# Compressing the cached pages of two sequences at a time, with the products spread over five steps

## The reference

```python
def compress(x, pe, w1, w2):              # CMP_LEN 32, CMP_STRIDE 16, hidden 128
    ch = x[:, :nch * CMP_STRIDE].reshape(N, nch, CMP_STRIDE, G, hd)
    hsum = 0
    for r in range(2):
        proj = jnp.einsum('ncsgd,sdh->ncgh', ch + pe[r][:, None, :], w1[r])
        hsum = hsum + proj[:, r:r + n_cmp]
    return jnp.einsum('ncgh,hd->ncgd', jax.nn.gelu(hsum), w2)
```

## Time and profile before

| | us |
|---|---|
| three timed runs | 1248.45, 1250.84, 1255.35 |
| their median | 1250.84 |
| the profiled execution, its own time | 1257.54 |
| its span, first to last instruction | 1255.7 |
| PE busy in the span | 1222.4 |

### The profile page before, as it was taken

How to read it: one execution, slowest core, us unless ns; L and a number is a source line. 1 busy time by engine, 2 the same in 40 slices (tenths; PEclk the granted TensorE clock), 3 DMA queues, 4 the chain that set the end, 5 groups by cost and what they waited for, 6 DMA issues and landing times.

```text
span 1255.7 us, 19647 instructions
## 1 busy us (share of the span) xinstructions
PE 1222.4 (97%) x6846; PEld 957.1 (76%) x6846; DVE 692.4 (55%) x1524; ACT 325.0 (26%) x736; POOL 281.0 (22%) x444
## 2 busy tenths in 40 slices
PE   6999999999999899999999999999999999999999
PEld 5787656878788666666787887688888888888887
DVE  6766363665655433132377724349777888873331
ACT  3422522444544422112131115221212112110000
POOL 4632002334333514214260210130101010000000
PEclk9999999999999899999999999999999999999999
DMA  6342475232333689998421731022222222302240
GB/s 228 147 175 68 138 262 184 84 103 68 89 110 128 208 300 356 305 313 306 169 102 40 296 135 34 34 68 83 85 84 84 85 69 87 143 30 93 92 159 18
DMA packets 83636, 174.59 MB, mean 139 GB/s; under 512 B 11377, under 2 KB 49074, under 8 KB 82642
## 3 DMA queue, kind: packets, MB, share of 16 engines
q1 hardware_dynamic: 67810, 123.79, 29.2%
q10 hardware_dynamic: 11568, 39.06, 8.4%
q0 software_dynamic: 4160, 10.49, 2.5%
HBM read 163.21 MB, written 10.09 MB: 138 GB/s over the span
## 4 chain that ended last, share of the span: by engine, by line
PE 89%; DVE 5%; issue 2%; ACT 2%; DMA 1%; POOL 1%; SPq 0%; ACTq 0%; DVEq 0%; POOLq 0%
PE ps L2963 20%; PE ps L3000 11%; PE ps L1865 10%; PE ps L661 7%; PE ps L1333 6%; PE ps L2674 6%; PE ps L2775 4%; PE ps L754 3%; PE ps L2687 3%; PE ps L1266 2%; PE ps L1238 2%; PE ps L1252 2%; PE ps L2823 1%; PE ps L653 1%; PE ps L1965 1%
## 5 line engine op out<-in xcount | busy, mean ns | idle before, releaser
L2963 PE MATMUL ps<-arena 128*128 128x272 f32 x1120 | 257.1, 392 | 0.7 <-DVE arena L3332 0.7
L2963 PEld LDWEIGHTS ps<-arena 128*128 128x128 f32 x1120 | 212.7, 190 | 44.9 <-DVE arena L3332 1.1
L1865 PE MATMUL ps<-arena 128*128 128x272 f32 x512 | 123.7, 399 | 0.5 <-PE ps L1965 0.5
L3000 PE MATMUL ps<-arena 128*128 128x272 f32 x528 | 121.8, 392 | 0.0
L1865 PEld LDWEIGHTS ps<-arena 128*128 128x128 f32 x512 | 97.0, 193 | 27.5 <-issue 8.3
L3000 PEld LDWEIGHTS ps<-arena 128*128 128x128 f32 x528 | 100.3, 190 | 20.7
L1333 PEld LDWEIGHTS ps<-arena 128*128 128x128 f32 x768 | 89.8, 195 | 11.9 <-issue 11.4
L1333 PE MATMUL ps<-arena 128*128 128x128 f32 (+1 forms) x768 | 95.6, 282 | 1.8 <-DVE arena L1460 1.8
L661 PE MATMUL ps<-arena 128*128 128x272 f32 x392 | 93.1, 399 | 3.4 <-POOL arena L462 3.4
L661 PEld LDWEIGHTS ps<-arena 128*128 128x128 f32 x392 | 75.2, 193 | 20.6 <-POOL arena L462 3.8
L2622 ACT ACTIVATE arena<-arena 128x560 f32<-128x560 f32 x44 | 35.3, 848 | 159.7 <-DVE arena L3347 152.9
(11 more groups left out here) (396 smaller groups left out, 1843.4 us busy)
## 6 DMA issues: line engine op xcount, KB each, us to landing
arena<-in_w_close SPq DMA_DIRECT2D x68, 512.0 KB, 3.4
arena<-in_pages_cmp SPq DMA_DIRECT2D x128, 128.0 KB, 2.1
arena<-in_past_va ACTq DMA_DIRECT2D x6, 2048.0 KB, 12.3
arena<-in_w_down SPq DMA_DIRECT2D x16, 704.0 KB, 6.0
arena<-in_past_ka ACTq DMA_DIRECT2D x6, 1792.0 KB, 10.7
arena<-in_w_close ACTq DMA_DIRECT2D x16, 512.0 KB, 6.7
arena<-in_w_proj SPq DMA_DIRECT2D x15, 512.0 KB, 3.8
arena<-in_pages_ks SPq DMA_DIRECT2D x96, 64.0 KB, 4.0
```

Of the source, the lines that this page charges most:

```text
L1865: last_one = pe.matmul(ps[:, gate_bank(q), 0:HALF], ring[:, n % CLOSE_RING, k * P:(k + 1) * P], m.h[:, k, half * HALF:(half + 1) * HALF], ...
L2963: last = pe.matmul(ps[:, bank(f, i), 0:HALF], w[:, k * P:(k + 1) * P], halved[:, rhs, k, :], start=(k == 0), stop=(k == 3))
L3000: last = pe.matmul(ps[:, down_bank(i, j), 0:HALF], w[:, k * P:(k + 1) * P], rhs[:, k, :], start=(k == 0), stop=(k == KH - 1))
```

## The change

One unit of compression is now two sequences with one `kv`: eight units for sixteen halves. A page transfer brings 64 KB (the 128 columns of one `kv`) and a unit takes 32 of them. Matmuls of EVEN and ODD have 256 columns, those of BOTH 252. ODD is accumulated on EVEN in the same half of bank 7. In between, ACT copies EVEN's result out (`take_even`) and POOL takes differences of its neighbours (`slopes`, new). `first` comes out of EVEN plus ODD by one ACT instruction (`take_first`), and `between` by two DVE instructions (`add`). The 24 matmuls of a unit are given to five steps, as 5, 3, 5, 5 and 8. Unit `n` begins in step 4 + 5n, the last ends in step 43. `bend` and `hidden` work on four rows at once. POOL's sums come in six instructions for a unit (four of 384 elements, two of 240), and stand behind the `bend` of the unit before; `next_sum` lies elsewhere. `w1` is loaded ahead of the first pages, after a wait for the prompt's last tile. The 32 page numbers of a pair of sequences are read into registers at once, ahead of the loads of its two units. Two constants of the samples' attention are loaded behind the compression, no longer ahead of the third sequence's pages.

```diff
-    chunked, next_sum = at(37944, 2, 8, 66), at(37944, 16, 64)
+    chunked, next_sum = at(37944, 2, 8, 66), at(45820, 16, 2, 64)
     w_both = at(43772, 2, 8, P)
     c_prob_t, c_score = at(39000, 2, T), at(40024, QT, 8, 32)
-    second, inner, bent = at(41048, 2, 2, P), at(41560, 2, 2, P), at(42072, 2, 2, P)
-    hid = at(42584, 2, 2, 2, P)
+    even, slope = at(41048, 4, 64), at(41304, 4, 64)
+    inner, bent = at(41560, 4, P), at(42072, 4, P)
...
-    copied = sem("sample_copied")
+    copied, slope_ready = sem("sample_copied"), m.x_root_ready
...
+
+    UNIT_STEPS = 5
+    PIECES = [[(EVEN, 0, 5)], [(EVEN, 5, 8)], [(ODD, 0, 5)], [(ODD, 5, 8), (BOTH, 0, 2)], [(BOTH, 2, 8)]]
+
+    def begin(n):
+        return 4 + UNIT_STEPS * n
+
+    def even_step(n):
+        return begin(n) + 1
+
+    def last_step(n):
+        return begin(n) + UNIT_STEPS - 1
+
+    def small_step(s):
+        return last_step(2 * (s // 2) + 1) + 3 + s % 2
+
+    def product_done(n, product):
+        return 1 + 3 * n + product + 1
...
+        return product_done(2 * (s // 2) + kv, BOTH)
...
-    def part(product):
-        return ps[:, PROJ, P * product:P * product + P].rearrange("p (g i) -> p g i", g=2)
-
-    def page_view(s, kv):
-        return pages[:, s % 2].rearrange("p n (v a w i) -> p v w a n i", v=2, a=16, w=2)[:, kv]
+    def slot(product):
+        at_ = 256 * (product == BOTH)
+        return ps[:, PROJ, at_:at_ + 256].rearrange("p (x i) -> p x i", x=4)
+
+    def page_view(n):
+        return pages[:, n % 2].rearrange("p n (a w i) -> p w a n i", a=16, w=2)
+
+    def windows(kv):
+        return hid[:, kv].rearrange("p x (i w) -> p w x i", w=2)
...
+        def pages_of(q):
+            found = []
+            for p4 in range(2 * NPAGE // 4):
+                at = 2 * q * NPAGE + 4 * p4
+                _, four = nc.values_load_multi_w_load_instructions(
                     table[0:1, at:at + 4], engines=(mybir.EngineType.SP,), min_val=0,
                     max_val=d["pages_cmp"].shape[0] - 1)
-                for c, page in enumerate(found):
-                    sp.dma_start(pages[:, s % 2, 4 * p4 + c, :],
-                                 d["pages_cmp"][ds(page, 1)].rearrange("a p n -> p (a n)"))\
-                        .then_inc(page_in[s % 2], 16)
+                found += four
+            return found
+
+        def load_pages(n, found):
+            _, kv = PAIRS[n]
+            for c, page in enumerate(found):
+                sp.dma_start(pages[:, n % 2, c, :],
+                             d["pages_cmp"][ds(page, 1), :, P * kv:P * kv + P].rearrange("a p n -> p (a n)"))\
+                    .then_inc(page_in[n % 2], 16)
...
         sp.wait_ge(m.z_full, m.products_done)
-        load_pages(0)
+        found = pages_of(0)
+        sp.wait_ge(m.tile_done, m.NJOB)
+        sp.dma_start(w1, d["w_cmp1"]).then_inc(w_in, 16)
+        load_pages(0, found)
         m.store_tiles(sp)
-        sp.dma_start(w1, d["w_cmp1"]).then_inc(w_in, 16)
         m.store_values(sp)
-        load_pages(1)
+        load_pages(1, found)
         sp.wait_ge(m.stored, 16 * 7)
         sp.wait_ge(m.h_scaled, QT + 1)
-        m.load_constants(sp)
-        for s in range(2, NSEQ):
-            sp.wait_ge(proj_full, products(s - 2, 1))
-            load_pages(s)
+        for n in range(2, len(PAIRS)):
+            if n % 2 == 0:
+                found = pages_of(n // 2)
+            sp.wait_ge(proj_full, product_done(n - 2, BOTH))
+            load_pages(n, found)
...
-        sums(*HALVES[0])
+        def sums(n):
+            pool.wait_ge(page_in[n % 2], 16 * 2 * NPAGE * (n // 2 + 1))
+            if n == 0:
+                pool.wait_ge(m.h_scaled, QT + 1)
+            else:
+                pool.wait_ge(proj_full, product_done(n - 1, BOTH))
+            x = page_view(n)
+            to = next_sum.rearrange("p a s (n i) -> p a (s n) i", i=4)
+            for a in range(0, 16, 4):
+                rows = slice(a, a + 4)
+                pool.tensor_tensor(to[:, rows, :, 0:3], x[:, 0, rows, :, 1:4], x[:, 1, rows, :, 0:3], ALU.add)
+            by_seq = x.rearrange("p w a (s n) i -> p w a s n i", s=2)
+            to = next_sum.rearrange("p a s (n i) -> p a s n i", i=4)
+            for a in range(0, 16, 8):
+                rows = slice(a, a + 8)
+                last = pool.tensor_tensor(to[:, rows, :, 0:NPAGE - 1, 3], by_seq[:, 0, rows, :, 1:NPAGE, 0],
+                                          by_seq[:, 1, rows, :, 0:NPAGE - 1, 3], ALU.add)
+            last.then_inc(chunked_ready, 1)
+
+        def slopes(n):
+            pool.wait_ge(second_ready, 2 + 2 * n + 1)
+            if n >= 1:
+                pool.wait_ge(proj_free, 2 + n)
+            pool.tensor_tensor(slope[:, :, 0:63], even[:, :, 0:63], even[:, :, 1:64], ALU.subtract)\
+                .then_inc(slope_ready, 1)
+
         for kv in range(2):
             bend(p_hid[:, kv, :, 0:C], p_inner[:, kv, :, 0:C], kv + 1)
-        for n, (s, kv) in enumerate(HALVES):
-            if n + 1 < len(HALVES):
-                sums(*HALVES[n + 1])
-            bend(hid[:, s % 2, kv, :, 0:NCMP_S], inner[:, kv, :, 0:NCMP_S], 2 + n + 1)
+        sums(0)
+        for n, (q, kv) in enumerate(PAIRS):
+            slopes(n)
+            if n >= 1:
+                pool.wait_ge(hid_ready, 2 + n)
+            bend(hid[:, kv, :, 0:NCMP_S], inner[:, :, 0:NCMP_S], 2 + n + 1)
+            if n + 1 < len(PAIRS):
+                sums(n + 1)
+        pool.wait_ge(proj_full, product_done(len(PAIRS) - 1, BOTH))
...
-            act.activation(bent[:, kv, :, 0:NCMP_S], inner[:, kv, :, 0:NCMP_S], ACT.Tanh, scale=GELU_IN)\
+        def take_even(n):
+            act.wait_ge(proj_full, product_done(n, EVEN))
+            if n >= 1:
+                act.wait_ge(slope_ready, SLOPE0 + n)
+            act.copy(even[:, :, :], slot(EVEN)).then_inc(second_ready, 1)
+
+        def take_first(n):
+            q, kv = PAIRS[n]
+            act.wait_ge(proj_full, product_done(n, BOTH))
+            if q >= 1:
+                act.wait_ge(s_full, s_index["small", 2 * q - 1] + 1)
+            act.activation(windows(kv)[:, 0], slot(ODD), ACT.Identity, bias=m.cmp_bias[:, kv:kv + 1])\
+                .then_inc(second_ready, 1)
+
+        def bend(n):
+            act.wait_ge(inner_ready, 2 + n + 1)
+            if n >= 1:
+                act.wait_ge(hid_ready, 2 + n)
+            act.activation(bent[:, :, 0:NCMP_S], inner[:, :, 0:NCMP_S], ACT.Tanh, scale=GELU_IN)\
                 .then_inc(bent_ready, 1)
 
...
+                    if small_step(s) == t:
                         small(s)
-                    for kv in range(2):
-                        if last_step(s, kv) + 1 == t:
-                            bend(s, kv)
-                for s in range(NSEQ):
-                    for kv in range(2):
-                        if last_step(s, kv) == t:
-                            second_half(s, kv)
+                for n in range(len(PAIRS)):
+                    if even_step(n) == t:
+                        take_even(n)
+                    if last_step(n) == t:
+                        take_first(n)
                 if 0 <= t - 2 < U:
                     take_turned(t - 2)
+                for n in range(len(PAIRS)):
+                    if last_step(n) + 1 == t:
+                        bend(n)
...
+        def piece(n, product, from_, to):
+            q, kv = PAIRS[n]
+            x = page_view(n).rearrange("p w (e s) n i -> p w s e n i", e=2)
+            follows = next_sum.rearrange("p (e s) q i -> p s e q i", e=2)
+            if from_ > 0:
+                pass
+            elif product == EVEN:
+                pe.wait_ge(proj_free, 2 + n)
+                if n >= 1:
+                    pe.wait_ge(second_ready, 2 + 2 * n)
+                pe.wait_ge(page_in[n % 2], 16 * 2 * NPAGE * (n // 2 + 1))
+            elif product == ODD:
+                pe.wait_ge(second_ready, 2 + 2 * n + 1)
+            else:
+                pe.wait_ge(chunked_ready, 10 + n + 1)
+            for s1 in range(from_, to):
+                if product == BOTH:
+                    out = slot(BOTH).rearrange("p (e q) i -> p e q i", e=2)[:, :, :, 0:63]
+                    last = pe.matmul(out, w_both[:, kv, s1, :], follows[:, s1, :, :, 0:63], start=(s1 == 0), stop=(s1 == 7))
+                else:
+                    last = pe.matmul(slot(product), w1[:, kv, product, s1, :], x[:, product, s1],
+                                     start=(product == EVEN and s1 == 0), stop=(s1 == 7),
+                                     skip_group_check=(product == ODD))
+            if to == 8:
                 last.then_inc(proj_full, 1)
...
-            pe.wait_ge(hid_ready, 2 + 2 * s + 2)
+            pe.wait_ge(hid_ready, 2 + 2 * (s // 2) + 2)
...
+                n, place = divmod(t - begin(0), UNIT_STEPS)
+                if 0 <= n < len(PAIRS):
+                    for product, s0, s1 in PIECES[place]:
+                        piece(n, product, s0, s1)
...
```

(50 more changed lines are left out.)

81 lines of the change are left out of this document (20 added, 61 removed).

## The result

The changed kernel takes 1268.62 us (median of 5 runs, 1256.08 to 1270.68) against 1253.23 for the kernel before (5 runs, 1248.45 to 1255.35). The ratio is 1.0111, with a 95% interval from 1.0087 to 1.0136: 1.1% slower, where the forecast was 1240, or 0.9% faster.

A forecast was written before the change was run, and what follows sets the result against it. PE's own work was taken to bound the kernel (busy 1222 of 1256 us). Products -7.0, loop waits 0, pages +0.5, loop end -7.2, late keys +2.7 gave -11.0: 1250.8 to 1239.8, forecast 1240; own range 1234 to 1244, all cases 1232 to 1251.

The forecast's parts named there:

- What is late next: Samples' attention behind the loop: PE 13.7 us earlier, SP's chain 2.7 earlier, 8.3 to spare; PE waits 2.7 for second keys.
- The third rival: SP's queue becomes the bound through slower page transfers, 17 us more, 1257; chance 0.08.
- The products: Compression matmuls on PE: 384 records at 0.216 us, 82.8 instead of 89.8, saving 7.0 us.
- The second rival: Wide operand or new waits eat the products' gain and the loop's end stays as it is: 1250; chance 0.22.
- Waits inside the loop: PE's gaps in the steady loop stay as before: 0 in the sum, between 3 us lost and 4.4 won.
- ODD's wait for `take_even`: In a unit's third step, where the second is 512 wide (steps 15 and 35): some 1.1 us, twice.
- the wait for `add`: PE's wait in the loop, 1.8 us in all, gets cheaper with 12 records ahead of it instead of 16 short ones.
- On DVE and ACT: Both engines in the loop: fewer instructions per unit than two halves had, busy about half the time, priced at nothing.
- The end of the loop: Around steps 43 and 44: PE's 2.6 us gap and the low clock's 4.6 us both go, saving 7.2 us.
- The pages, the stores, `w1`: Page waits at units 4 and 6 cost 0.5 us; moved stores and earlier `w1` ahead of the loop cost nothing.
- SP's pace in the loop: SP's issues and number reads for a pair of sequences take 43 us, against 45.4 for two units.

The follow-up runs named there:

- the long execution: Trace of the changed kernel rerun with nothing edited, the shortest execution of that rerun; span 1261.4 us.
- 8: Changed kernel with 32 page numbers of the samples' attention read into SP's registers ahead of the wait for unit 6; 1253.38 us, ratio 1.0009.
- 11: Changed kernel without POOL's four large sums in units 1 to 7 (output not the reference's); 1257.53 us, ratio 1.0046.
- 7: Kernel before, with SP's loads for the samples' attention made to wait for the scores of step 40; 1266.25 us, ratio 1.0095.
- 3: Changed kernel with `small`, the last products of a sequence, one step later; 1262.11 us, ratio 1.0058.
- 2: Changed kernel with POOL's sums of a unit in two instructions instead of six; 1275.03 us, ratio 1.018.
- 4: Changed kernel with a unit's 24 matmuls as three whole products, in its first, third and fifth step; 1266.78 us, ratio 1.0107.
- 9: Changed kernel with `small` one step later and the 32 page numbers of the samples' attention read ahead; 1247.93 us, ratio 0.9971.
- 12: Kernel before, with the 32 page numbers of the samples' attention read ahead of the wait for the products; 1251.56 us, ratio 1.0001.
- 5: Changed kernel with the second keys issued ahead of the last 16 pages of the samples' attention; 1262.79 us, ratio 1.0071.
- 6: Changed kernel with `small` one step later and the second keys ahead of the last 16 pages; 1256.66 us, ratio 1.0028.
- 10: Changed kernel with `small` one step later, second keys ahead of the last 16 pages, and 32 page numbers read ahead; 1247.33 us, ratio 0.9957.
- experiment 1: Changed kernel run again, nothing edited; 1267.12 us, ratio 1.0125.

## Why the prediction was wrong

**The step that failed is "What is late next".** It had the right object, the second keys, and the right form, spare time against two shifts, and it gave 2.7 us. All three numbers were off. PE was to come 13.7 us earlier and came 4.6 earlier (3.4 in the long execution). SP's chain was to start 2.7 us earlier, because seven units would save 6.1; it started 5.3 later (6.5 in the long execution), since the loop up to step 38 saved nothing and unit 6 ends a step later. And the landing was taken as 8.6 us whatever else was under way, while it was 14.0 when the keys were issued at 445.08. There POOL issues a window of past values (`past_vw`, 1024 KB) ahead of them, at 444.39, ACT issues the third keys at 446.50, and the pages of values on SP's queue come from 447.98; the timeline has

```profile
444.39 0.76 POOL L1767 DMA_DIRECT2D arena<-in_past_vw  x1 [3.26 <-PE ps L1929]
...
445.08 0.43 SPq L1715 DMA_DIRECT2D arena<-in_past_ka  x1
...
446.50 0.39 ACTq L1715 DMA_DIRECT2D arena<-in_past_ka  x1
...
447.98 3.90 SPq L1708 DMA_DIRECT2D arena<-in_pages_v  x5
```

The traces of all kernels part by this order, with the same 1792 KB each time (in us, of issue and from issue to landing):

| trace | `past_vw` issued | second keys issued | landed after |
|---|---|---|---|
| before | 447.78 | 435.71 | 8.4 |
| changed | 443.23 | 441.68 | 8.4 |
| 8 | 445.92 | 440.13 | 9.3 |
| 11 | 440.13 | 439.07 | 9.4 |
| changed, long | 444.39 | 445.08 | 14.0 |
| 7 | 444.71 | 445.73 | 14.1 |
| 3 | 439.64 | 440.73 | 14.8 |

2 and 4 belong to the long ones (14.7 and 14.2), 9 and 12 to the short ones (9.6 and 8.4). Both `past_vw` and the third keys are released by PE's products. So a PE that comes earlier not only uses up the spare time, it also brings other transfers on top of the late one. In 5, 6 and 10, where SP's own sixteen pages follow the keys directly, the landing is 15.1, 14.9 and 12.2 us, so `past_vw` is not the only company that counts. No run moves `past_vw` alone, so that it is the cause is read from these orders and not tried.

PE was ready at 459.17 - 8.99 = 450.2. With the landing of before it would have waited to 445.1 + 8.6 = 453.7, or 3.5 us; the other 5.5 are the longer landing. The wait and the clock behind it cost 11.3 us in that trace and 13.7 to 14.2 in medians (8 and 9). The third rival had named SP as the bound and a time of 1257, but for the pages of the compression: PE waited 0 us for those in the changed kernel, where 0.5 was forecast, and 0.5 and 1.1 in 8 and 11. The right queue was named at the wrong place, and given 8%. (Its 17 us count from the forecast of 1240, so they are 6 beyond the gain and not 17.)

**The products** were to save 7.0 and saved 2.0 (88.6 to 86.6 us). The distance of 0.216 was right. The error is in comparing two counts that end differently. The 5.61 of a half before has the change to other work behind each piece in it (48 records at 0.1118 are 5.37 us, measured are 5.54). L653's 3.45 has none, it is 16 x 0.2155, and with it the 82.8 had none. A unit pays some 0.1 us for each of its five pieces, 10.82 instead of 10.34, and 82.8 became 86.6. The second rival's bound of 1.5 was nearer, but by luck: the distance of 0.230 that it rests on is not there.

**Waits inside the loop** were put at 0 over those of before, and cost some 5.8. ODD's wait for `take_even`, for which I had worked out 1.1 us twice, was none in the changed kernel and 1.4 us, in two, where `small` came later (3, 6, 9 and 10); the wait for `add` stayed (1.8 before, 2.0 now) instead of getting cheaper. What came was a wait that the prediction doesn't list: `small` for `hidden`, 0.9 us in two before and now 5.5 in three, and a stretch of low clock behind the last. The timeline of the changed kernel around that one:

```profile
367.83 0.63 ACT L1229 ACTIVATE arena<-arena 128x508 f32<-128x508 f32 x1
...
371.23 2.03 POOL L1147 TENSOR_TENSOR arena<-arena 128x240 f32<-128x240 f32 x2
371.26 1.04 DVE L1469 TENSOR_TENSOR arena<-arena 128x2 f32<-128x2 f32 x1
...
372.33 1.82 DVE L1474 TENSOR_SCALAR arena<-arena 128x384 f32<-128x384 f32 x2
...
374.07 0.68 DVE L1528 SCALAR_TENSOR_TENSOR arena<-arena 128x508 f32<-128x508 f32 x1
...
374.90 0.68 PE L1401 MATMUL ps<-arena 128*128 128x127 f32 x4 [2.57 <-DVE arena L1528]
...
375.83 4.03 PE L1391 MATMUL ps<-arena 128*128 128x256 f32 x10
```

A DVE instruction on two elements takes 1.04 us beside POOL's sum and 0.16 otherwise (the one at 375.28); `weigh` stands behind it, `hidden` behind `weigh`, and PE behind `hidden`. What `hidden` needs from ACT and POOL was there long before: the last of it, L1229, ended at 368.5. The next ten records of the products take 4.03 us at the lower clock, where the ten at 364.88 took 2.43. "On DVE and ACT a unit has fewer instructions than two halves had [...] so I price that at nothing" is the sentence that failed: the instructions were fewer and 10.7 us longer. Experiments 3 and 9 give the price of the consequence (5.0 and 5.5), 11 gives its cause.

**The end of the loop** was right as a mechanism: the gap of 2.6 us and the low clock at 414 are gone. The size was that of the one execution traced: its low stretch was 10.2 us long, while the trace of 12 has 3.4 there. So 2.6 + 1.7 = 4.3 is what a common execution could save, not 7.2. The forecast said that the trace lay 6.7 above the median and took the same 11.0 from both; that trace's long low stretch accounts for 1.6 of the 6.7 (29.5 us against 27.9 in the table), a saving that the median doesn't offer.

**The pages, the stores, `w1`** and SP's pace in the loop were right: no wait of PE for `in_pages_cmp`, and none for POOL's sums. A page of 64 KB lands 1.9 us after its issue, and SP issues 17 in 9.76 us from 370.18 on, one in 0.57 us, so they overlap. The Trainium skill (DMA: Bandwidth & Descriptors, Bandwidth) lists 0.95 us for 64 KB, measured there with GpSimd as the issuer; read as time that each transfer has for itself, it would have bound the loop, and the trace speaks against that reading.

**The new sum.** -2.0 for the products, +5.8 for `small` and `hidden`, -4.3 for the end of the loop, 0 for pages, +11.3 to +14 for keys and pages behind the loop: +10.8 to +13.5. Measured are +14.5 (experiment 1) and +15.4 (the result). Without the two causes the sum is -6.3, and experiment 9 has -4.4.

**What stays open:** the remaining 1 to 5 us. Low stretches near 223 and 237 us hold up to 3.4 of them in one trace, and the longer executions of the changed kernel, at clocks of 0.983 to 0.989, have no trace. Why one of the eleven executions of the changed kernel, and two of the ten in experiment 3, are some 10 us shorter is known in part: in the trace of the short one the keys were issued 1.5 us ahead of `past_vw`, in the long one 0.7 behind it. That the transfers share the engines is argued from these orders, 376 to 406 GB/s and a share of 1.03 to 1.06. The hour of the issue alone doesn't tell: 440.13 was early enough in 8, and 440.73 too late in 3, where PE's work and the transfers that it releases came some 6 us earlier.

## What to carry to other kernels

For every transfer behind a changed stage, write down when it is issued, when it lands and when it is wanted, and treat the spare time as the thing at risk: here an earlier queue was worth nothing to a kernel that had 8 us to spare, and the same queue started 5 to 9 us later cost 13 to 14. Ask also which other transfers an earlier engine will release beside it. Take the length of repeated matmuls from the first record to the next instruction's first, since every piece pays its own change to other work (some 0.1 us here). And ask of each trace whether its low-clock stretches are there in a common execution before a saving is read from them.

## What the runs showed of the hardware

- VectorE's instructions got longer beside GpSimd's sums: `weigh`'s mean is 497 ns before (two sums for a half), 664 with six for a unit, 760 with two large ones, 553 without the large ones.
- The same transfer of 1792 KB landed 8.4 us after its issue at 441.68, with 1024 KB on another queue issued 1.5 us behind it, and 14.0 after 445.08, with these issued 0.7 us ahead.
- Around a wait of 9.0 us, from 450.2, the TensorE clock was at its lower level (1.2 GHz) for 10.2 us from 451.7, and around two waits of 4.0 and 3.4 for 17.1. In 8, 9 and 10, without such waits, there was no such stretch.
- Reading page numbers costs SP some 30% of its time in this chain: 16 issues took 13.6 us with their numbers read in between, and 9.5 without (13.0 and 8.4 in the kernel before and experiment 12).
